# The third mixer's differential attention: masks moved to TensorE, scores and exponentials of the next head moved ahead of the difference

## The reference, cut to what matters

```python
s = jnp.einsum('bqhcd,bkhcd->bhcqk', q_blk, k) * scale        # c = 0, 1
mask = kpos[None, :] <= qpos[:, None]
p = jax.nn.softmax(jnp.where(mask, s, NEG_BIG), axis=-1)
a = p[:, :, 0] - lam * p[:, :, 1]
return jnp.einsum('bhqk,bkhe->bqhe', a, v)
```

## Time and profile before

| | us |
|---|---|
| median of 3 runs | 2163.68 (2160.76 to 2164.32) |
| profiled execution | 2161.74 |
| its span | 2159.8 |
| PE busy | 2094.8 (97%) |
| DVE busy | 1086.7 (50%) |
| ACT busy | 753.6 (35%) |
| the mixer: first scores start / last `apply` ends, from the start of the span | 1548.3 / 1622.3 |

### The profile page before, as it was taken

The page is one execution under the profiler, slowest core; times in us unless marked ns, Lnnn a source line. Parts: engine busy times, 40 slices in busy tenths (PEclk is TensorE's granted clock), DMA queues, the critical chain, the costliest instruction groups (busy, mean ns, idle before and its releaser), DMA issues.

```text
span 2159.8 us, 28677 instructions
## 1 busy us (share of the span) xinstructions
PE 2094.8 (97%) x11739; PEld 1732.1 (80%) x11739; DVE 1086.7 (50%) x1393; ACT 753.6 (35%) x1045; POOL 220.1 (10%) x196
## 2 busy tenths in 40 slices
PE   7999999999999999999999999999879999999998
PEld 7887788888888888867888888888668878888886
DVE  4764655554354453353655354466565445454453
ACT  6444433532221332475422122332454243122221
POOL 3000220400000130000400000232201000000001
PEclk9999999999999999999999999999999999999999
DMA  6231000222222322002222222334212202222221
GB/s 243 80 116 40 20 22 34 85 98 98 97 97 97 117 79 97 20 21 78 78 98 98 97 97 97 117 118 143 82 43 95 95 27 94 98 98 97 97 97 59
DMA packets 28336, 186.99 MB, mean 87 GB/s; under 512 B 3536, under 2 KB 3664, under 8 KB 6480
## 3 DMA queue, kind: packets, MB, share of 16 engines
q1 hardware_dynamic: 25200, 173.48, 22.4%
q0 software_dynamic: 2320, 11.01, 1.5%
q10 hardware_dynamic: 720, 1.11, 0.1%
HBM read 181.39 MB, written 2.10 MB: 85 GB/s over the span
## 4 chain that ended last, share of the span: by engine, by line
PE 89%; DVE 6%; ACT 4%; issue 1%; DMA 0%; POOL 0%; ACTq 0%; DVEq 0%; POOLq 0%
PE PS L561 88%; ACT Y L1420 2%; DVE Y L2112 1%; DVE WL L2115 1%; ACT WH L1420 1%; DVE Y L2115 1%; DVE DMX L2746 1%; DMA MX<-mem_t 0%; DVE SQ L2115 0%; DVE HL L2112 0%; PE PS L777 0%; ACT ABUF L1420 0%; DVE HL L2115 0%; DVE PS L2115 0%; ACT SQ L1420 0%
## 5 line engine op out<-in xcount | busy, mean ns | idle before, releaser
L561 PE MATMUL PS<-HH,WH 128*128 128x512 f32 x1544 | 606.7, 393 | 3.4 <-DVE HL L2115 2.1
L561 PE MATMUL PS<-HH,WL 128*128 128x512 f32 x1544 | 601.2, 389 | 0.0
L561 PE MATMUL PS<-HL,WH 128*128 128x512 f32 x1544 | 590.6, 389 | 0.0
L2115 DVE TENSOR_TENSOR WL<-STG,WH 128x2048 fp32r<-128x2048 f32 (+1 forms) x159 | 358.6, 2256 | 277.0 <-ACT WH L1420 276.9
L1420 ACT ACTIVATE WH<-STG 128x2048 fp32r<-128x2048 f32 (+2 forms) x167 | 307.3, 1840 | 520.8 <-PE PS L561 520.8
L561 PEld LDWEIGHTS PS<-HH,WH 128*128 128x128 f32 x1544 | 289.9, 188 | 69.1 <-issue 6.1
L561 PEld LDWEIGHTS PS<-HH,WL 128*128 128x128 f32 x1544 | 289.9, 188 | 60.5
L561 PEld LDWEIGHTS PS<-HL,WH 128*128 128x128 f32 x1544 | 290.0, 188 | 59.0 <-issue 0.2
L561 PE MATMUL PS<-UPH,WH 128*128 128x512 f32 x832 | 324.2, 390 | 1.4 <-DVE UPL L2112 1.4
L561 PE MATMUL PS<-UPH,WL 128*128 128x512 f32 x832 | 323.7, 389 | 0.0
L561 PE MATMUL PS<-UPL,WH 128*128 128x512 f32 x832 | 323.7, 389 | 0.0
(11 more groups left out here) (304 smaller groups left out, 2132.8 us busy)
## 6 DMA issues: line engine op xcount, KB each, us to landing
STG<-weights SPq DMA_DIRECT2D x159, 1024.0 KB, 4.8
KEY_STG<-weights POOLq DMA_DIRECT2D x4, 1024.0 KB, 6.0
XT<-x_t SPq DMA_DIRECT2D x2, 1024.0 KB, 8.7
KEY_X<-mem_t POOLq DMA_DIRECT2D x2, 1024.0 KB, 6.5
out_t<-Y SPq DMA_DIRECT2D x8, 256.0 KB, 2.0
STG<-weights SPq DMA_DIRECT2D x4, 256.0 KB, 5.4
MX<-mem_t ACTq DMA_DIRECT2D x4, 256.0 KB, 7.2
CON<-consts SPq DMA_DIRECT2D x1, 1024.0 KB, 9.0
```

Of the source, the lines that this page charges most:

```text
L561: return pe.matmul(o, l, r, start=start, stop=stop, **kw)
L2115: return dve.tensor_tensor(o, a, b, op)
```

## The change

The causal mask becomes a product. `MASK` holds an identity and the additive mask, and each diagonal square gets one more accumulating product of 128 columns. The scores are split in two groups with a semaphore each, and every group is followed by its masks. The first group is map 0 and block 1 of map 1 (it shares a PSUM bank with block 1 of map 0); the second is the rest of map 1. The step `top(h+1,0)` stands before `difference(h)`, `exponentials(h+1,0)` before the first `turned_weights(h,0)`, and memory quarter r is computed and emptied one head earlier.

```diff
+            MASK = sb("MASK", [P, 2, P], F32R, scope=sc)
...
-                def scores(h):
...
+                def mask(c, b):
+                    o = score_at(c, b) + b * P
+                    return mm(PSF[:, o:o + P], MASK[:, 0, :], MASK[:, 1, :], False, True, skip_group_check=True)
+
+                def first_scores(h):
+                    if h:
+                        pe.wait_ge(sems["df_exp"], 8 * h - 4)
+                    for b in (3, 2, 0):
+                        score(h, 0, b)
+                    if h:
+                        pe.wait_ge(sems["df_exp"], 8 * h - 3)
+                    score(h, 0, 1).then_inc(sems["df_b"], 1)
+                    for b in (3, 2, 0):
+                        mask(0, b)
+                    pe.wait_ge(sems["df_b"], h + 1)
+                    score(h, 1, 1)
+                    mask(0, 1)
+                    mask(1, 1).then_inc(sems["df_s"], 1)
+
+                def second_scores(h):
                     if h:
                         pe.wait_ge(sems["df_exp"], 8 * h)
...
+                    for b in (3, 2, 0):
+                        score(h, 1, b)
+                    for b in (3, 2, 0):
+                        last = mask(1, b)
+                    last.then_inc(sems["df_s1"], 1)
...
-                scores(0)
+                pe.wait_ge(sems["late_in"], 5)
+                first_scores(0)
+                second_scores(0)
                 pooled(0)
                 pooled(1)
                 memory_part(0, 0)
+                memory_part(0, 1)
                 pooled(2)
                 pooled(3)
                 for h in range(4):
                     if h < 3:
-                        scores(h + 1)
+                        first_scores(h + 1)
                     pe.wait_ge(sems["df_a"], 4 * h + 4)
                     if h == 0:
                         pe.wait_ge(sems["mixed"], 4)
                     turn(h, 0)
-                    memory_part(h, 1)
+                    if h < 3:
+                        second_scores(h + 1)
                     turn(h, 1)
                     apply(h, 0)
+                    if h < 3:
+                        memory_part(h + 1, 0)
                     turn(h, 2)
                     apply(h, 1)
+                    if h < 3:
+                        memory_part(h + 1, 1)
                     apply(h, 2)
-                    if h < 3:
-                        memory_part(h + 1, 0)
...
+            A(MASK[:, 0, :], con("ident"), ACT.Copy).then_inc(sems["late_in"], 1)
+            A(MASK[:, 1, :], con("causal_add"), ACT.Copy).then_inc(sems["late_in"], 1)
...
             exponentials(0, 0)
             exponentials(0, 1)
+            memory_values(0)
...
             for h in range(4):
+                if h < 3:
+                    exponentials(h + 1, 0)
                 turned_weights(h, 0)
                 turned_weights(h, 1)
-                if h < 3:
-                    exponentials(h + 1, 0)
-                memory_values(h)
                 turned_weights(h, 2)
                 if h < 3:
                     exponentials(h + 1, 1)
+                    memory_values(h + 1)
                     split_hi(R0["C.mem"] + h + 2)
...
-                tt(three, three, con("causal_add").unsqueeze(1).to_broadcast([P, 3, P]), ALU.add).then_inc(sems["df_mask"], 1)
-                tt(one, one, con("causal_add"), ALU.add).then_inc(sems["df_mask"], 1)
-                dve.wait_ge(sems["df_mask"], 4 * h + 2 * c + 2)
-                for b in range(NB):
-                    last = dve.tensor_reduce(DMX[:, c, 0, b:b + 1], ...)
+                dve.wait_ge(sems["df_s1" if c else "df_s"], h + 1)
+                for b, cc in ((0, 1), (2, 1), (3, 1)) if c else ((1, 1), (0, 0), (1, 0), (2, 0), (3, 0)):
+                    last = dve.tensor_reduce(DMX[:, cc, 0, b:b + 1], ...)
...
-            difference(0)
             for h in range(4):
                 if h < 3:
                     top(h + 1, 0)
+                difference(h)
+                if h < 3:
                     top(h + 1, 1)
-                    difference(h + 1)
                 split_lo(R0["C.mem"] + h + 2)
```

More of the change, by code:

```diff
@@ L105 @@
 SEMAPHORES = """
-at bc bg bg_tr bt cb_zero const_in conv conv0 df_a df_at df_bc df_exp df_g df_mask df_max
+at bc bg bg_tr bt cb_zero const_in conv conv0 df_a df_at df_bc df_exp df_g df_max df_s1
 df_nm df_o df_r0 df_ri df_rs df_rt df_s df_sq df_ss df_tr df_w d_exp
@@ L1182, in layer_c_mixer, with score @@
             def layer_c_mixer():
-                def scores(h):
+                def score(h, c, b):
+                    return mm(PSF[:, score_at(c, b):score_at(c, b) + DF_WID[b]], QC[64 * c:64 * c + 64, h, b * P:(b + 1) * P],
+                              KC[64 * c:64 * c + 64, h, 0:DF_WID[b]], (c, b) in ((0, 1), (0, 2), (0, 3), (1, 2), (1, 3)), False,
+                              skip_group_check=True)
+                def mask(c, b):
[16 more added lines that the diff above has]
+                def second_scores(h):
                     if h:
                         pe.wait_ge(sems["df_exp"], 8 * h)
[L1186 to L1192, removed]
+                    for b in (3, 2, 0):
[3 more added lines that the diff above has]
+                    last.then_inc(sems["df_s1"], 1)
                 def pooled(g):
@@ L2037, in exponentials @@
             def exponentials(h, c):
-                act.wait_ge(sems["df_nm"], 2 * h + 2)
+                act.wait_ge(sems["df_nm"], 2 * h + c + 1)
                 if c:
@@ L2043, in exponentials @@
                     act.wait_ge(sems["df_tr"], 3 * h - 3)
-                for b in range(NB):
+                for b in (1, 0, 2, 3):
                     o, n = DF_OFF[b], DF_WID[b]
@@ L2734, in top @@
             def top(h, c):
[L2736 to L2741, removed]
-                tt(three, three, con("causal_add").unsqueeze(1).to_broadcast([P, 3, P]), ALU.add).then_inc(sems["df_mask"], 1)
-                tt(one, one, con("causal_add"), ALU.add).then_inc(sems["df_mask"], 1)
-                dve.wait_ge(sems["df_mask"], 4 * h + 2 * c + 2)
-                for b in range(NB):
-                    last = dve.tensor_reduce(DMX[:, c, 0, b:b + 1], PSF[:, score_at(c, b):score_at(c, b) + DF_WID[b]], AX.X, ALU.max)
+                dve.wait_ge(sems["df_s1" if c else "df_s"], h + 1)
+                for b, cc in ((0, 1), (2, 1), (3, 1)) if c else ((1, 1), (0, 0), (1, 0), (2, 0), (3, 0)):
+                    last = dve.tensor_reduce(DMX[:, cc, 0, b:b + 1], PSF[:, score_at(cc, b):score_at(cc, b) + DF_WID[b]], AX.X, ALU.max)
                 last.then_inc(sems["df_max"], 1)
```

## The result

The changed kernel takes 2194.10 us (median, 2191.56 to 2194.76) against 2163.38 for the kernel before: ratio 1.0142, 95% interval 1.0130 to 1.0154. That is 30.7 us slower. Forecast were 2182.3 and a range of 2174 to 2188: the sign was right, the size was not.

What follows compares the result with a forecast made beforehand. PE was taken as the bound outside the mixer, with the chain changing engines inside it. Profiled 2161.7 plus 12.2 for the new order plus 6.5 for clock gave 2180.4; the median stands 1.9 above, so 2182.3 us, range 2174 to 2188.

Steps and rivals of the forecast that it cites:

- The order of the queues: Mixer, DVE: difference(h) behind top(h+1,0) makes PE wait at least 4.8 us before the turn.
- a second loop: Mixer: last memory part, memory values, split_hi, split_lo, maxima, difference; next first turn at T + 9.9, period 20.5 us.
- Idle stretches: PE ahead of each first turn in the mixer: four idle stretches of 5 to 7.7 us, ended by the difference.
- The sum at full clock: Mixer end at 1634.4 against 1622.2, so 12.2 us longer without clock losses.
- the period that was forecast: Distance from one head's first turn to the next in the mixer: 20.5 us.
- The 6.2 of idle time: PE in the second loop: work for 3.5 of 9.9 us, so idle for about 6.2.
- Masks at no loss on TensorE: Mask products on PE at 0.11 us each, 0.9 per head; DVE loses 2 x 0.76 of masks per head.
- Pairs: Scores on PE: the new order leaves no pair, so 4.3 us instead of 2.36, 1.9 more per head.
- The step that failed: PE clock behind four idle stretches in the mixer: 1.6 us lost for each, 6.5 in all, ends 0 and 10.
- The 4.9 us of low clock: Third half-clock stretch before the change: ran on 4.9 us after PE resumed from 5.56 idle, costing up to 2.45.
- rival C: Clock stays at half for the whole burst behind each idle stretch: 27 us more, 2209; chance 0.04.
- Rival A: top(h+1,0) falls into DVE's 5.3 us idle time and PE becomes the bound: 4.4 us faster, 2159.3; chance 0.06.

Runs made afterwards that it cites:

- e7: e4 with one exchange on VectorE, difference(h) behind top(h+1,0) instead of ahead of it: 2179.9 us, ratio 1.0078 to the kernel before.
- e3: Changed kernel with one exchange on ScalarE, split_hi of the next weight quarter ahead of memory_values: 2188.6 us, ratio 1.0112 to the kernel before.
- e1: Changed kernel with unread 128-row fp32r products filling TensorE's wait for the difference: 2181.4 us, ratio 1.0080 to the kernel before.
- e4: Kernel before with only the masks moved to TensorE, as products behind the eight paired scores: 2158.4 us, ratio 0.9971.
- e9: Kernel before with only the eight scores of a head reordered so that they do not pair: 2167.6 us, ratio 1.0017.
- e2: Changed kernel with unread 64-row f32 products filling TensorE's wait for the difference: 2190.2 us, ratio 1.0111 to the kernel before.
- e5: Changed kernel with memory_part(h+1,0) right behind the first turn, ahead of the second scores: 2186.1 us, ratio 1.0110 to the kernel before.
- e6: Changed kernel with all eight scores of a head in paired order ahead of the first turn, masks behind: 2183.7 us, ratio 1.0090 to the kernel before.
- e10: e4 with memory parts one head earlier, memory_values behind split_hi, and two idle stretches filled with unread 128-row products: 2153.4 us, ratio 0.9952 to the kernel before.

## Why the prediction was wrong

Right, point by point:

- The order of the queues. The difference behind `top(h+1,0)` keeps PE from the turn (e7), and the memory values, split and `split_lo` are a second loop (chain above, e3). Idle stretches were forecast at 5.1 and some 6.2, then 7; they are 4.7, 5.2, 5.2 and 6.9.
- The sum at full clock. It had 12.2 us on 73.9, so 86.1. e1, the same order with the clock held, measures 88.3. The 2.2 between them is spread: 1.2 at the entry, where both groups of scores and masks were priced too low and all steps stand in a row, and 0.2 to 0.3 in each head, where the second group is on the path. The changed kernel's own first period agrees: 24.73 less half of the 8.5 us of work at half clock is 20.5, which is the period that was forecast. (The 6.2 of idle time in the prediction is a slip: 9.9 less 3.5 is 6.4. It does not enter the sum.)
- Masks at no loss on TensorE, 0.12 each in a row of eight (e4) and 0.16 in rows of three; the taken 0.11 was near. The Trainium skill's 81 ns for such a product ("TensorE: Matmul & The Clock Gate", back-to-back issue gap) is below both.
- Pairs. That their loss costs is right, and 1.9 us per head was too low. In the changed kernel the four scores of map 0 alone take 2.35 us (1590.62 to 1592.97), as long as all eight did in pairs. At full clock, in e1, the eight take 2.35 + 0.63 + 1.92 = 4.9 us instead of the 4.3 of the forecast, and the eight masks 1.15 instead of 0.9:

```profile
1582.01 2.42 PE L562 MATMUL PS<-KC,QC 64*128 64x512 f32 x8
1584.36 0.55 PE L562 MATMUL PS<-MASK 128*128 128x128 f32 x3
1584.84 0.70 PE L562 MATMUL PS<-KC,QC 64*128 64x256 f32 x2
1585.47 0.44 PE L562 MATMUL PS<-MASK 128*128 128x128 f32 x2
...
1591.72 1.99 PE L562 MATMUL PS<-KC,QC 64*128 64x512 f32 x6
1593.64 0.55 PE L562 MATMUL PS<-MASK 128*128 128x128 f32 x3
1594.03 0.62 PE L1248 MATMUL PS<-CON,Y 128*128 128x128 f32 x4
```

  The second group, 2.31 us instead of 2.05, is on the path; the first is mostly hidden behind the split. The rule of the Trainium skill on packing ("TensorE: Matmul & The Clock Gate", Part 3, packing small matmuls) agrees, with 2.36 against 3.76 us in e9.

The step that failed is the clock: "I take 1.6 for each, 6.5; ends 0 and 10". It measures 15.8 (e1 against the changed kernel), beyond even the far end, and 12.2 + 15.8 + 2.2 is the 30.1 of the mixer, to rounding. (In this sum, as in the forecast, the kernel before keeps its own losses to the clock.) The term was read from two low stretches of 3.4 us that lay in dense memory parts. Even those were read too kindly: the clock was not back 3.4 us after dense work started, but 4.3 (1580.07 to 1584.4) and 4.0 (1611.09 to 1615.1). And the term was carried over to places where PE does other work: behind a turn now come 64-row scores without pairs, masks and transposes. e2 shows that 64-row f32 products did not hold the clock up, e5 and e6 that moving them away from behind the turn gives 7.0 and, with the columns, 12.4 us. The 4.9 us of low clock after PE resumed was taken as the worst case because it was the worst row. In that row PE was busy without a wait, with pooled products and then scores, behind 5.56 us of idle time: of the three it was the one most like the places to come, and even its price, 2.45 each, gives only the 10 of the far end.

The forecast's rival C, the clock at half for a whole burst, had 27 us more and a chance of 0.04. The truth lay between: half of 7.4 to 10.6 us, so up to 3.7 to 5.3 us behind each idle stretch, against the 1.6 that were taken and the 10.6 of rival C. Rival A (the early maxima fall into idle time of VectorE) is out: in the changed kernel and in e7 PE waits for the difference ahead of every first turn, for 4.3 us or more.

What stays open: which property of the 64-row f32 scores counts, why the clock fell at different times in idle stretches that are alike (the 10.2 us of e5, e4 against e7), and the spread of the times of e1 beyond its clock.

## What to carry to other kernels

Moving an instruction ahead on an in-order engine moves all its waits ahead of what it passes; before a step is put in front of another, ask when its input is issued, and on the other engine behind what. Here one exchanged pair on VectorE cost 21 us, while two parts of the same change, masks as products and the early memory part, were gains of 3.6 and 2.7 us of mixer, the first mostly through the clock.

Price an idle stretch of TensorE by what stands around it, not by its length alone: what it costs is half of the time that PE works before the clock is back. Here that was up to 5.3 us behind one idle stretch, and filling the stretches with 128-row products that nobody reads took 15.8 us (e1) and some 3 us (e10) off the mixer.

## What the hardware showed unexpectedly

- An idle time of 1.60 us, and one of 1.06, behind 3.7 us of 64-row f32 products was followed by half clock for 6.8 us (e2); an idle time of 1.45 us behind 16 products of 128 rows was not (e1).
- At idle stretches of 4.3 to 4.9 us the low stretch was 3.4 us in e7 and 10.2 us in the changed kernel with 4.7. At the same 3.98 us of idle time with the same PE instructions up to there, it was 3.4 us in e4 and 6.8 us in e7.
